# Two-block transformer kernel: at five group boundaries the next group's third weight chunk gets a buffer of its own and is loaded and split ahead of the first

## The reference

```python
x = x + 0.5 * rms_norm(swiglu(rms_norm(x, g_ffn1_pre[l]), wg, wu, wd), g_ffn1_post[l])
mixed = hybrid_mixer(rms_norm(x, g_mix_pre[l]), w_in[l], ..., w_out[l], ...)
x = x + rms_norm(mixed, g_mix_post[l])
x = x + 0.5 * rms_norm(swiglu(rms_norm(x, g_ffn2_pre[l]), wg, wu, wd), g_ffn2_post[l])
```

## Time and profile before

| what | us |
|---|---|
| runs | 2138.7, 2140.26, 2140.29; median 2140.26 |
| the profiled execution | 2139.68 |
| its span, first to last instruction | 2137.8 |
| busy: PE / DVE / ACT / POOL | 2066.9 / 1169.3 / 997.4 / 281.7 |
| mean granted clock of TensorE over the span | 0.985 |

### The profile page before, as it was taken

The page is one execution under the profiler, slowest core; times in us unless marked ns, Lnnn a source line. Parts: engine busy times, 40 slices in busy tenths (PEclk is TensorE's granted clock), DMA queues, the critical chain, the costliest instruction groups (busy, mean ns, idle before and its releaser), DMA issues.

```text
span 2137.8 us, 27911 instructions
## 1 busy us (share of the span) xinstructions
PE 2066.9 (97%) x11878; PEld 1798.2 (84%) x11878; DVE 1169.3 (55%) x1102; ACT 997.4 (47%) x1074; POOL 281.7 (13%) x193
## 2 busy tenths in 40 slices
PE   7789999999999999999999989999999999999998
PEld 6679999998999998887877878887887787777886
DVE  5455445654454545455555865545554556676453
ACT  5544434334354335435445645445444535646443
POOL 3103421304234300001200001001000210001000
PEclk8889999999999999999999999999999999999999
DMA  7224556532455555555543436555555553345553
GB/s 192 71 87 159 176 177 207 170 127 99 138 177 170 170 174 195 180 189 165 179 156 117 139 137 205 188 178 170 183 181 187 168 177 126 107 164 169 179 182 113
DMA packets 195137, 343.64 MB, mean 161 GB/s; under 512 B 14058, under 2 KB 97292, under 8 KB 194908
## 3 DMA queue, kind: packets, MB, share of 16 engines
q1 hardware_dynamic: 194388, 339.73, 48.2%
q0 software_dynamic: 368, 0.79, 0.2%
q10 hardware_dynamic: 280, 1.66, 0.2%
HBM read 341.10 MB, written 1.05 MB: 160 GB/s over the span
## 4 chain that ended last, share of the span: by engine, by line
PE 82%; DVE 7%; ACT 6%; DMA 3%; issue 1%; POOL 0%; SPq 0%; DVEq 0%; POOLq 0%
PE banks L472 15%; PE banks L475 15%; PE banks L473 15%; PE banks L316 9%; PE banks L318 9%; PE banks L317 9%; PE banks L367 3%; DVE w_lo L309 2%; ACT w_hi L302 2%; PE banks L1547 2%; DMA raw<-w_in 1%; ACT e L2227 1%; PE banks L511 1%; DMA raw<-ffn_wg 1%; DVE hT L715 1%
## 5 line engine op out<-in xcount | busy, mean ns | idle before, releaser
L309 DVE TENSOR_TENSOR w_lo<-raw,w_hi 128x2048 fp32r<-128x2048 f32 x321 | 750.8, 2340 | 605.0 <-ACT w_hi L302 604.8
L302 ACT ACTIVATE w_hi<-raw 128x2048 fp32r<-128x2048 f32 x321 | 613.6, 1913 | 688.9 <-DMA raw<-ffn_wd 150.7
L472 PE MATMUL banks<-w_hi,xn_hi 128*128 128x512 f32 x1248 | 494.1, 396 | 11.0 <-DVE w_lo L309 10.6
L473 PE MATMUL banks<-w_lo,xn_hi 128*128 128x512 f32 x1248 | 487.9, 391 | 0.0
L475 PE MATMUL banks<-w_hi,xn_lo 128*128 128x512 f32 x1248 | 482.8, 391 | 0.0
L316 PE MATMUL banks<-xn_hi,w_hi 128*128 128x272 f32 x1104 | 323.9, 293 | 7.4 <-DVE xn_lo L423 7.4
L318 PE MATMUL banks<-xn_hi,w_lo 128*128 128x272 f32 x1104 | 320.8, 291 | 0.0
L317 PE MATMUL banks<-xn_lo,w_hi 128*128 128x272 f32 x1104 | 319.4, 289 | 0.0
L472 PEld LDWEIGHTS banks<-w_hi,xn_hi 128*128 128x128 f32 x1248 | 235.5, 189 | 62.4 <-DVE w_lo L309 14.2
L475 PEld LDWEIGHTS banks<-w_hi,xn_lo 128*128 128x128 f32 x1248 | 235.4, 189 | 50.0
L473 PEld LDWEIGHTS banks<-w_lo,xn_hi 128*128 128x128 f32 x1248 | 235.6, 189 | 46.7
(11 more groups left out here) (333 smaller groups left out, 2505.1 us busy)
## 6 DMA issues: line engine op xcount, KB each, us to landing
raw<-w_in SPq DMA_DIRECT2D x60, 1024.0 KB, 5.2
raw<-ffn_w_gu SPq DMA_DIRECT2D x44, 1024.0 KB, 5.1
raw<-ffn_wd SPq DMA_DIRECT2D x44, 1024.0 KB, 4.8
raw<-ffn_wg SPq DMA_DIRECT2D x40, 1024.0 KB, 5.1
raw<-ffn_wu SPq DMA_DIRECT2D x40, 1024.0 KB, 5.0
raw<-ret_w_in SPq DMA_DIRECT2D x24, 1024.0 KB, 5.1
raw<-ffn_w_down SPq DMA_DIRECT2D x22, 1024.0 KB, 4.9
raw<-ret_w_out SPq DMA_DIRECT2D x8, 1024.0 KB, 4.9
```

The lines of the kernel that those rows point to most:

```text
L302: nc.scalar.activation(w_hi[:, n0 % SLOTS, :], raw[:, n0 % SLOTS, :], ACT.Copy).then_inc(S["w_hi"], 1)
L309: nc.vector.tensor_tensor(w_lo[:, n0 % SLOTS, :], raw[:, n0 % SLOTS, :], w_hi[:, n0 % SLOTS, :].bitcast(F32), ALU.subtract).then_inc(S["w_ ...
L472: pe.matmul(ps[:, (b + n) * 512:(b + n + 1) * 512], xh, h, start=start, stop=False)
L473: pe.matmul(ps[:, (b + n) * 512:(b + n + 1) * 512], xh, o, start=False, stop=False)
```

## The change

Each seam's c2 (five chunks, listed in `EXTRA`) leaves the ring. It has a slot of its own: `raw_x`, `lo_x` in the same bytes, and `hi_x`, 16 KB per partition behind the seam's buffers in Y, with semaphores of its own (`raw_xin`, `x_hi`, `x_lo`).

- SP (`sp_extra`) issues its load behind the last load of the group before and ahead of c0's, on the condition that PE is done with chunk c2 - 9.
- ACT and DVE split it ahead of c0, while PE is at the end of the group before: in a feed-forward ahead of the last two splits, in the mixer in the order 2, 3, 6, 4, 5 counted from wout's first chunk, where 6 is c2. The split between the tiles in `act_post` and `dve_post` is gone.
- The ring's slot of c2 stays empty for one turn: c6 waits for chunk c2 - 4 in place of c2 (`slot_before`), behind c5 in SP's order. `slot_count` and `ring_count` number the landings and the splits accordingly, and PE waits through `wait_split`.

The diff, cut to its core (the calls that pass `ahead` lose that argument, and products read `hi_of(n0)`, `lo_of(n0)`; for DVE the places are those of ACT):

```diff
+EXTRA = [BASE[_n] + 2 for _n in ("mix0", "gu3", "gu4", "mix1", "gu5")]
...
+def slot_before(n0):
+
+    n = n0 - SLOTS
+    return n - SLOTS if n in EXTRA else n
...
+        extra_at = y_at + 4 * 7 * D
+        raw_x, lo_x, hi_x = (place(name, [P, CH], dt, extra_at + off) for name, dt, off in
+                             (("raw_x", F32, 0), ("lo_x", F32R, 0), ("hi_x", F32R, 4 * CH)))
...
-            if n0 >= SLOTS:
-                e.wait_ge(S["pe_chunk"], n0 - SLOTS + 1 + 4 * i)
+            if n0 in EXTRA:
+                e.wait_ge(S["pe_chunk"], n0 - 8)
+            elif n0 >= SLOTS:
+                e.wait_ge(S["pe_chunk"], slot_before(n0) + 1 + 4 * i)
...
             for c in range(2 * 11 + NDN):
+                if c == 2 * 11 + NDN - 2 and f < 5:
+                    split_hi(base + 2 * 11 + NDN + 2, 0)
                 if c or f == 2:
                     split_hi(base + c + AHEAD, 0)
...
             for kt in range(5, KT):
                 fill_hi(kt, 0)
-            if ahead:
-                split_hi(ahead, 0)
             for kt in range(KT):
                 fill_hi(kt, 1)
...
-            wide_straight(act, BASE[f"wout{l}"], 4, split_hi)
+            for k in (2, 3, 6, 4, 5):
+                split_hi(BASE[f"wout{l}"] + k, 0)
...
+        def sp_extra(name, w):
+            c = MIX_COLS[1] if name.startswith("mix") else 0
+            load(sp, BASE[name] + 2, 0, w.rearrange("(k p) c -> p k c", p=P)[:, 0:4, c:c + 512], (4, 512))
...
                 sp_xffn(2 + 2 * l, a["ffn1_wg_2"][l], a["ffn1_wu_2"][l], a["ffn1_wd_2"][l])
+                sp_extra(f"mix{l}", a["w_in_2"][l])
                 sp_m2(l)
+                sp_extra(f"gu{3 + 2 * l}", a["ffn2_wu_2"][l])
                 sp_xffn(3 + 2 * l, a["ffn2_wg_2"][l], a["ffn2_wu_2"][l], a["ffn2_wd_2"][l])
+                if l + 1 < LAYERS:
+                    sp_extra("gu4", a["ffn1_wu_2"][l + 1])
```

More of the change, by code:

```diff
@@ L139, with ring_count, slot_count @@
 BOTH = [BASE["out0"] + 2, BASE["out0"] + 3] + [BASE[f"gu{_f}"] + _c for _f in (2, 3, 4, 5) for _c in (20, 21)]
+EXTRA = [BASE[_n] + 2 for _n in ("mix0", "gu3", "gu4", "mix1", "gu5")]
+def ring_count(n0):
+    return n0 + 1 - sum(x < n0 for x in EXTRA)
+def slot_count(n0):
+    if n0 in EXTRA:
+        return EXTRA.index(n0) + 1
+    return n0 // SLOTS + 1 - sum(x < n0 and x % SLOTS == n0 % SLOTS for x in EXTRA)
+def slot_before(n0):
+    n = n0 - SLOTS
+    return n - SLOTS if n in EXTRA else n
 POST_END = [BASE[_n] + dict(PLAN)[_n] for _n in ("dn2", "wout0", "dn3", "dn4", "wout1", "dn5")]
@@ L492, in quarter @@
             def quarter(n0, u, q, tb, fill):
-                b, slot = ring(f, u) + tb, n0 % SLOTS
-                pe.wait_ge(S["w_lo"], n0 + 1)
+                b = ring(f, u) + tb
+                wait_split(n0)
                 for i in range(4):
@@ L499, in quarter @@
                     w = slice(i * 512, (i + 1) * 512)
-                    last = token_product(b, tok(xn_hi, kt, tb), tok(xn_lo, kt, tb), [w_hi[:, slot, w]], [w_lo[:, slot, w]],
+                    last = token_product(b, tok(xn_hi, kt, tb), tok(xn_lo, kt, tb), [hi_of(n0)[:, w]], [lo_of(n0)[:, w]],
                                          kt == 0, kt == KT - 1)
@@ L651, in dve_xffn @@
             for c in range(2 * 11 + NDN):
+                if c == 2 * 11 + NDN - 2 and f < 5:
+                    split_lo(base + 2 * 11 + NDN + 2, 0)
                 if c or f == 2:
@@ L758, in sp_xffn @@
             for c in range(20):
+                if base + c in EXTRA:
+                    continue
                 g, q = c // 4, c % 2
@@ L1799, in quarter @@
                 n0 = base + 2 * g + q
-                b, slot = mix_bank(l, g) + tb, n0 % SLOTS
-                pe.wait_ge(S["w_lo"], n0 + 1)
+                b = mix_bank(l, g) + tb
+                wait_split(n0)
                 for i in range(4):
```

60 lines of the change are left out of this document (37 added, 23 removed).

## The result

| | us, median of the runs | runs |
|---|---|---|
| before | 2140.28 | 4, 2138.70 to 2140.78 |
| changed | 2123.02 | 4, 2122.94 to 2124.40 |

The ratio of the changed kernel to the one before is 0.9921 (95% interval 0.9909 to 0.9934), 17.3 us less. The forecast was 2123.6 us, between 2121.4 and 2128.5.

What follows compares the result with a forecast made beforehand. The kernel was taken as a stream of PE matmuls (82% of the chain), losing time where PE waits at five seams. 11.9 (c2) + 1.0 (c3) + 3.1 (slow clock) = 16.0 us off 2139.68 gave 2123.6, range 2121.4 to 2128.5.

Steps and rivals of the forecast that it cites:

- The wait for c2 (11.9 us): At five seams of the second block, PE stops waiting for c2's low half: 5 x 2.38 = 11.9 us gained.
- c3 (1.0 us): At three of five seams, PE's wait for c3's low half goes: 3 x 0.34 = 1.0 us gained.
- the room at c4: At a seam, chunk c4 is still ready 1.5 us before PE reads it, so it costs nothing.
- What is added, at nothing: Before each seam, one extra load, activation and subtraction cost nothing, hidden by PE's last products; worst-case landing 10.4 us after issue.
- The spells (3.1 us): Half-clock stretches behind third and fifth seams vanish with PE's wait for c2: 2 x 1.57 = 3.1 us gained.
- The spell in the merge: In the second mixer's merge at 1907, a half-clock stretch stays; were it gone too, the clock gain would be 4.7 us.
- The sum: Whole kernel: 11.9 + 1.0 + 3.1 = 16.0 us off the profiled 2139.68, giving 2123.6; chance 0.62.
- Slower by a late load: At each seam, c2's extra load lands late and holds ACT's splits and the norm's first square: 2144 us, chance 0.02.
- The 12 us: Room at a feed-forward seam from the extra load's issue to the latest harmless landing, at 976.4.
- The wait moves on to c3 or c4: At the seams PE waits for c3 or c4 instead: 2125.6 us, at most 2136; chance 0.11.
- The change doesn't do what it says: At SP the load is held until its former time and the split waits where it stood: 2139 and more, chance 0.03.
- The upper end of the range: 2128.5 us for the kernel: both half-clock stretches at the seams stay and 2 us is given back at c3.

Runs made afterwards that it cites:

- The late load: The changed kernel with c2's load issued behind c1's and its split still ahead of c0's: 2167.50 us, 1.0135 of the kernel before.
- changed again: The changed kernel timed once more, with nothing altered, on another chip: 2123.53 us, 0.9919 of the kernel before.
- c6 late: The changed kernel, but c6's load waits until PE is done with c2, as before the change: 2122.99 us, 0.9921 of the kernel before.
- the table early: The changed kernel with ACT's load of the root's table ahead of c0's split at the two seams behind w_out: 2121.80 us, ratio 0.9914.

## Why the prediction was right, and where it was off

**The wait for c2 (11.9 us): right.** The five waits went. With the slot but the split in its old place all of them are back, and divided over the two kinds of seam the gain adds up.

**c3 (1.0 us) and the room at c4: right.** 1.1 and 1.5 us in hand, as forecast to a tenth.

**What is added, at nothing: right, with less in hand than it may seem.** The five extra loads took 7.1 to 8.4 us from issue to landing, between the 5.2 of one load and the worst case of 10.4. At the third seam ACT waited 0.53 us for the landing, and the cover held. The late load shows what the term would have been without it.

**The spells (3.1 us): right as to the seams, with the mechanism now tested.** A spell followed the 2.1 us wait in 7 of 9 seams into a feed-forward and in none of the 40 seams where that wait was gone or 1.55. The order of the products differs too where it is 1.55; but the 18 waits of 1.3 to 1.6 us for ysb, with the order as it was, drew no spell either. By the Trainium skill ("TensorE: Matmul & The Clock Gate", section "Why this matters for your kernels") none of these gaps should have mattered, and the spells should have stayed. The runs decide for the wait and against that rule as I applied it. My reading that it was luck which of the five seams had a spell was too coarse: into a mixer the same wait had no spell in six. Nor is the length of one wait all: in the merge, where the five spells came, the single waits are about 1 us and less.

**The spell in the merge.** I left it where it was. The changed kernel's first profiled execution has none, its second (changed again) has one, and so have c6 late and the table early: it comes and goes with nothing of the seams changed. It cost less than a spell at a seam: the stretch from the fourth to the fifth seam gave 3.63, which leaves 0.9 for it beside c2 and c3, and the same stretch took 278.79 us in changed again, with the spell, and 277.84 without. PE waits there part of the time in any case, which may be why; that was not tried.

**The sum.** 16.0 were forecast on a profiled execution, 17.4 came from the second block: 0.9 of the difference is the spell of the merge, which was luck. The other 0.5 is some 0.1 in each of the other stretches and stays open; the waits for ysb do not give it, for they were 7.8 us in all before and 8.0 after. Of the medians the gain was 17.3, so 1.3 more than forecast; the base, a profiled execution 0.6 under the median of before, took half of that back, and the forecast was 0.6 too high. That it came so near the median is in part luck: two differences of opposite sign.

**The rivals.** *Slower by a late load*: its mechanism holds at 8.2 us of PE for 7.7 us of lateness. The 12 us are counted from the load's issue and not what was to spare: 3.5 us were, at the third seam. The sentence that nothing in the profile takes 16 us to land is wrong as it stands: one load of a table (cst<-tab_c) took 18.1 us in the kernel before, but at the kernel's start and with none of the weights. *The wait moves on to c3 or c4*: it did not. *The change doesn't do what it says*: it did. The upper end of the range is 0.2 low by its own terms, 2123.6 + 3.1 + 2.0 = 2128.7; nothing hangs on it.

## What to carry to other kernels

When an engine splits or converts the next operand in the middle of a latency chain, look first at whether the wait is for data or for program order; in this kernel a buffer of its own paid only because it let the work leave that place, and a reordering without memory gave some two fifths. A short stall of the matmul engine may cost more than itself: here a wait of 2.1 us was followed by a stretch at half clock, which costs 1.57 us, in 7 of 15 cases, and a wait of 1.55 in none of 5. Before an operation is put ahead in a strictly ordered engine, compute the latest landing that it stands: beyond it, each microsecond was paid in full here.

## What was not expected of the hardware

The 2.1 us wait of PE was followed by a spell of half clock in 7 of 9 seams into a feed-forward and in 0 of 6 into a mixer, though the idle time and the number of products around it are alike. No run tells the two apart, and it stays open. POOL's subtraction of 128x2048 fp32 took 4.61 us (2.29 on DVE), and beside it one xn_lo on DVE took 0.95 us in place of 0.35; DVE's own low half of c3 takes 2.85 beside POOL's additions in place of 2.29. The Trainium skill, in "GPSIMD Engine Reference", section "Specifications", says that GpSimd shares its SBUF interfaces with VectorE and names contention with instructions of two SBUF inputs; this trace agrees.
